# A two-layer decoder trunk on one core: GpSimd computes seven of the residue halves of the first weights

## The reference

```python
for layer in range(DEPTH):                                   # DEPTH = 2
    mod = cond @ ada_w[layer] + ada_b[layer]                 # cond = silu(c), 2048 -> 6*2048
    sh1, sc1, g1, sh2, sc2, g2 = jnp.split(mod[:, None, :], N_MOD, axis=-1)
    h = rms_norm(x) * (1.0 + sc1) + sh1
    # layer 0: block attention and differential attention; layer 1: window attention
    y = even_mixer(h, ...) if layer % 2 == 0 else odd_mixer(h, ...)
    x = x + g1 * y
    h = rms_norm(x) * (1.0 + sc2) + sh2
    x = x + g2 * swiglu(h, ffn_w_in[layer], ffn_w_out[layer])
return rms_norm(x, final_norm)
```

## Time and profile before

| | |
|---|---|
| time, median of 3 runs | 2230.98 us (2230.1 to 2231.77) |
| the profiled execution: time | 2232.42 us |
| the profiled execution: span | 2230.3 us |
| mean granted TensorE clock | 0.993 of full speed |
| busy: TensorE, VectorE, ScalarE, GpSimd | 97%, 73%, 44%, 0% of the span |
| chain that ended last: TensorE, VectorE, DMA, ScalarE | 86%, 8%, 3%, 2% of the span |

### The profile page before, as it was taken

The page is one execution under the profiler, slowest core; times in us unless marked ns, Lnnn a source line. Parts: engine busy times, 40 slices in busy tenths (PEclk is TensorE's granted clock), DMA queues, the critical chain, the costliest instruction groups (busy, mean ns, idle before and its releaser), DMA issues.

```text
span 2230.3 us, 26268 instructions
## 1 busy us (share of the span) xinstructions
PE 2158.4 (97%) x10012; PEld 1787.4 (80%) x10012; DVE 1621.0 (73%) x1698; ACT 977.9 (44%) x1281; POOL 9.4 (0%) x21
## 2 busy tenths in 40 slices
PE   4789999999999999999999999999999999999998
PEld 3578888878888888888887888878888888888886
DVE  6989898988789988777668666587665545455546
ACT  4344444454443444434445444464443444434444
POOL 0000000000000000000000000000000000000000
PEclk9899999999999999999999999999999999999999
DMA  9978779859889999977755533348765555555543
GB/s 397 421 293 317 306 303 375 349 232 364 335 328 373 380 379 376 368 293 291 283 213 211 195 128 118 132 180 321 282 246 206 191 189 190 189 198 194 189 151 151
DMA packets 82559, 593.06 MB, mean 266 GB/s; under 512 B 9424, under 2 KB 9584, under 8 KB 10912
## 3 DMA queue, kind: packets, MB, share of 16 engines
q1 hardware_dynamic: 81216, 587.31, 68.3%
q0 software_dynamic: 1248, 4.44, 0.7%
HBM read 589.62 MB, written 2.10 MB: 265 GB/s over the span
## 4 chain that ended last, share of the span: by engine, by line
PE 86%; DVE 8%; DMA 3%; ACT 2%; DVEq 1%; issue 0%; SPq 0%; ACTq 0%
PE ps L1386 26%; PE ps L1388 26%; PE ps L1387 26%; PE ps L1374 3%; DVE w_lo L823 2%; DVE ada_raw L827 1%; DMA ada_raw<-in_ada 1%; DMA gate<-in_ada 1%; PE ps L1481 1%; PE ps L1414 1%; PE ps L1416 1%; PE ps L1415 1%; PE ps L1480 1%; DVE xT_lo L942 1%; DMA raw<-in_ab_in 0%; PE ps L1498 0%
## 5 line engine op out<-in xcount | busy, mean ns | idle before, releaser
L823 DVE TENSOR_TENSOR w_lo<-raw,w_hi 128x1024 fp32r<-128x1024 f32 x728 | 881.0, 1222 | 460.3 <-ACT w_hi L488 455.6
L488 ACT ACTIVATE w_hi<-raw 128x1024 fp32r<-128x1024 f32 x728 | 764.6, 1061 | 970.9 <-PE ps L1388 805.3
L1386 PE MATMUL ps<-w_hi,xT_hi 128*128 128x512 f32 x1940 | 768.8, 396 | 30.5 <-DVE xT_lo L1087 28.4
L1388 PE MATMUL ps<-w_hi,xT_lo 128*128 128x512 f32 x1940 | 760.3, 392 | 0.0
L1387 PE MATMUL ps<-w_lo,xT_hi 128*128 128x512 f32 x1940 | 759.7, 392 | 0.0
L1386 PEld LDWEIGHTS ps<-w_hi,xT_hi 128*128 128x128 f32 x1940 | 367.3, 189 | 109.7 <-DVE xT_lo L1087 30.6
L1388 PEld LDWEIGHTS ps<-w_hi,xT_lo 128*128 128x128 f32 x1940 | 366.9, 189 | 78.0
L1387 PEld LDWEIGHTS ps<-w_lo,xT_hi 128*128 128x128 f32 x1940 | 367.4, 189 | 74.2
L827 DVE SCALAR_TENSOR_TENSOR ada_raw<-ada_raw,cond 128x2048 f32<-128x2048 f32 x176 | 401.9, 2284 | 7.1 <-DMA ada_raw<-in_ada 5.6
L1386 PE MATMUL ps<-w_hi,hT_hi 128*128 128x512 f32 x896 | 351.7, 392 | 1.1 <-DVE work L1281 1.1
L1388 PE MATMUL ps<-w_hi,hT_lo 128*128 128x512 f32 x896 | 349.0, 390 | 0.0
(11 more groups left out here) (182 smaller groups left out, 954.8 us busy)
## 6 DMA issues: line engine op xcount, KB each, us to landing
ada_raw<-in_ada SPq DMA_DIRECT2D x176, 1024.0 KB, 6.6
raw<-in_ffn_in SPq DMA_DIRECT2D x176, 1024.0 KB, 4.9
raw<-in_ffn_out SPq DMA_DIRECT2D x88, 1024.0 KB, 5.0
raw<-in_ab_in SPq DMA_DIRECT2D x48, 1024.0 KB, 9.0
raw<-in_swa_in SPq DMA_DIRECT2D x20, 1024.0 KB, 4.8
raw<-in_ab_out SPq DMA_DIRECT2D x16, 1024.0 KB, 7.5
raw<-in_swa_out SPq DMA_DIRECT2D x16, 1024.0 KB, 4.8
spare<-in_ada SPq DMA_DIRECT2D x8, 1024.0 KB, 8.9
```

The lines of the kernel that those rows point to most:

```text
L488: nc.scalar.activation(w_hi[:, p % PAIRS, :, :], raw[:, t % RAW, 2 * (p % 2):2 * (p % 2) + 2, :], ACT.Copy).then_inc(hi_ready, 1)
L823: tt(w_lo[:, p % PAIRS, :, :], raw[:, (p // 2) % RAW, 2 * (p % 2):2 * (p % 2) + 2, :], w_hi[:, p % PAIRS, :, :].bitcast(F32), ALU.subtract ...
L1386: mm(out, hi[:, kt, tok], w_hi[:, q % PAIRS, k, :], start=(kt == 2 * ps0), stop=False)
L1388: last = mm(out, lo[:, kt, tok], w_hi[:, q % PAIRS, k, :], start=False, stop=(kt == 2 * ps1 - 1))
```

## The change

In steps 1 to 7 of the opening the third residue, of pair 3j-1 (pairs 2, 5, ..., 20), is computed by GpSimd and no longer by VectorE. GpSimd starts each as soon as ScalarE has written the upper half, and counts in a semaphore of its own, `lo_pool`. VectorE waits at the old place for that count, and passes it on to `lo_ready` with an instruction that moves no data, so that `lo_ready` still counts in order.

```diff
@@ -309,6 +309,7 @@
         hi_ready = sem("hi_ready")
         lo_ready = sem("lo_ready")
+        lo_pool = sem("lo_done_by_pool")
         pair_used = sem("pair_used")
@@ -452,6 +453,10 @@
             pool.dma_start(ada_bias[:, :, :, :], T["ada_bias"]).then_inc(s_bias, 16)
+            for p in range(2, 21, 3):
+                pool.wait_ge(hi_ready, AB0.pair(0, p) + 1)
+                nc.gpsimd.tensor_tensor(w_lo[:, p % PAIRS, :, :], raw[:, (p // 2) % RAW, 2 * (p % 2):2 * (p % 2) + 2, :],
+                                        w_hi[:, p % PAIRS, :, :].bitcast(F32), ALU.subtract).then_inc(lo_pool, 1)
             pool.wait_ge(ada_landed[START_SLOTS - 1], 16 * (START_TILES // START_SLOTS))
             pool.wait_ge(x0T_done, 8)
@@ -1097,7 +1102,8 @@
                 start_tile(4 * j + 2)
                 if j:
-                    lo(AB0, 0, 3 * j - 1)
+                    dve.wait_ge(lo_pool, j)
+                    nc.vector.engine_nop().then_inc(lo_ready, 1)
                 if j == 7:
                     lo(AB0, 0, 21)
```

## The result

| | before | changed |
|---|---|---|
| median of 11 executions each | 2231.43 us (2230.1 to 2232.96) | 2236.79 us (2235.81 to 2239.3) |
| profiled execution: time, span | 2232.42, 2230.3 us | 2236.53, 2234.4 us |

The ratio is 1.0029, with a 95% interval of 1.0022 to 1.0036. The medians are 5.4 us apart, where the forecast had 6.1. The forecast stood on a median of three executions, 2230.98 us, and the median of eleven is 2231.43: that 2237.1 comes within 0.3 us is partly luck, since the base was 0.45 us too low and the difference 0.7 us too high.

The account below looks back on a forecast made before the run. VectorE and transfers together bound the opening before TensorE's start. Each step grows 2.28 - 1.14 + 0.08 = 1.22 us; seven make 8.5, less 2.4 of waits: 2230.98 + 6.1 = 2237.1 us, range 2229.5 to 2240.8.

Parts of the forecast that it names:

- What bounds the opening: Before TensorE's start at 127.59 us, VectorE and the DMA transfers are both full; VectorE has some 0.2 us spare in 27.5.
- GpSimd's duration, 2.28 us: Each GpSimd subtraction of 128 x 1024 takes 2.28 us, VectorE's time for 2048 elements; bounds 1.14 and 3.42 us.
- The standstill b, the whole of it: In each step VectorE stands still for GpSimd's whole subtraction, 2.28 us; the other end was 0.
- The count, 0.08 us: VectorE's added instruction that moves no data takes 0.08 us, seven times, at the third residue's old place.
- The waits used up, 2.4 us: VectorE's 2.4 us of waits for landings in the opening are used up before the longer steps cost time.
- Landings don't slip: In the opening, transfers take 11.49 us to land, 4.9 unqueued, so issues may be 6.6 us late without landings moving.
- The sum: Seven steps, each 1.22 us longer, give 8.5 us; less 2.4 of waits, TensorE's start at 127.59 comes 6.1 us later.
- The rival of free overlap: VectorE and GpSimd run side by side in the opening: no change or at best 1 us faster, 2229.9 us; chance 0.30.
- the constants still land at 132.2: Behind the opening, under free overlap, the constants land at 132.2 us, leaving about 1 us of cover for TensorE.
- not even a VectorE without any residue could gain more than 2.05 us: At the opening's end: the last tile lands about 120.5 us, so at most 2.05 us, 0.09%, can be gained.
- the range of 8 in 10: Whole-kernel time with 8 in 10 chance: 2229.5 us (free overlap) to 2240.8 us (standstill of 2.8 us).
- the forecast's own: The forecast's own range of whole-kernel time, standstill of 2.04 to 2.8 us: 2235.4 to 2240.8 us; chance 0.50.

Follow-up runs that it names:

- e1_nobody: The changed kernel without GpSimd's seven subtractions, so nobody computes those lower halves: 2233.29 us, 2.3 us over the kernel before.
- e2_fill: The changed kernel with GpSimd filling 128 x 3072 unused elements with zeros in place of each subtraction: 2233.32 us, 2.3 us over the kernel before.
- e9: Against the kernel before: nobody computes the seven lower halves, and VectorE waits behind the opening for only three constants: 2228.54 us, 2.5 us less.

## Why the prediction was right

**What bounds the opening:** right. VectorE and the transfers were both full; nobody doing the seven residues left the gate tile of step 6 at 107.95, and seven standstills moved it to 112.57.

**GpSimd's duration, 2.28 us:** right, 2.3 and, where it could be seen without a wait, 2.36. That VectorE's rate for 2048 elements fitted is luck in part: it was borrowed from another engine. The Trainium skill (GPSIMD Engine Reference, Elementwise — side-by-side cycle accounting) has 4497 ns for twice the elements; the estimate of 2.25 us from it agrees with the trace.

**The standstill b, the whole of it:** right, 2.15 to 2.19 us in all 25 steps, of five kernels, in which VectorE's second lower half meets GpSimd's subtraction. It was a choice when I made it, with ScalarE's rows speaking for the other end; another engine's overlap said nothing about GpSimd's.

**The count, 0.08 us:** about 0.01 (95.09 to 97.31 is 2.22 us, a tile's usual 2.21). A step thus costs 2.16 - 1.14 + 0.01 = 1.03 us, not 1.22, and seven cost 7.2.

**The waits used up, 2.4 us:** nearly. They fell to 0.5. (Of the 2.4, 0.2 lie at 19.5 us, ahead of everything that the change touches; the 0.2 us ahead of the gate tile of step 6, from 107.62 to 107.84, which no row lists, make up for them.)

**"Landings don't slip":** this step failed in part. The gate tile of step 6 waited 0.53 us for a landing, and the rate fell to 375 GB/s. I had taken the room from a gate transfer, 11.49 us; the transfers into spare had 7.2 to 8.7 us from issue to landing at that place before, and 6.9 to 7.9 after, so they had little to give. While VectorE stands still, no slot comes free: in the changed kernel SyncE issues nothing between 91.91 and 97.41 us, and then spare, two raw transfers and gate by 99.63. The gate transfer lands 15.1 us after the issue into spare (14.8 before), so it takes over the delay of spare's issue.

**The sum:** 7.2 - 2.4 + 0.5 = 5.3 us, and 0.4 for waits on ScalarE that a landing had covered before, make 5.7; the restart moved by 5.8. The forecast's 6.1 has two errors that partly cancel: its step was 0.19 us too long (0.12 for the standstill, 0.07 for the count), 1.3 us in seven, and it had nothing for the 0.5 and 0.4 us of waits.

**The rival of free overlap** had the wrong price: 2229.9, where e1_nobody and e2_fill have 2233.3. The failed step is "the constants still land at 132.2": they landed at 134.5, behind a transfer issued 1 us earlier. Its sign was wrong too, since they are slower than before by 2.3 us. And "not even a VectorE without any residue could gain more than 2.05 us" looked at the restart alone, and VectorE's wait for the constants costs something too: e9 gained 2.5 us, though only about 1.6 of them by the residues. Had the engines overlapped freely, the time would have been near 2233 and still inside the range of 8 in 10, though not in the forecast's own.

**What stays open:** why seven executions of the changed kernel lie at 2235.8 to 2237.3 us and four at 2238.7 to 2239.3. The one profile is of the lower group. Why the raw transfers hold up the constants is read from the order of issue and not isolated.

## What to carry to other kernels

Before work goes from VectorE to GpSimd, look at what VectorE does at that moment: two SBUF inputs there and a reading instruction here run one after the other, and the move can pay only if GpSimd takes less time than it frees (2.16 us here for 1.14). The sign is a VectorE instruction of unusual length, not idle time. And where transfers pace an engine, freeing the engine gains only what lies behind the last landing, and may be taken back by a transfer that is now issued earlier, ahead of one that somebody waits for.

## What the runs showed of the hardware

GpSimd's fill of 128 x 3072 float32 takes 2.66 us, and one of 128 x 1024 takes 0.97. Its copy of 128 x 1024 held VectorE for 0.83 us, its subtraction for 2.16. Both engines' waits for each other are booked as busy time: 4.31 us of GpSimd for 2.3 of work, 3.37 us of VectorE for 1.22. So engines do not meet only at semaphores, as it says ahead of the prediction: these two also meet where they read. The Trainium skill (GPSIMD Engine Reference, Instruction dispatch) has about 6 us of loading for the first call of a freshly loaded kernel. The trace doesn't show it as a longer first subtraction (4.33 us, the other six 4.31 to 4.33). It may lie in the 28.7 us of GpSimd's idle time ahead of it, in which the library is selected; no run here shows when.
